# Two transformer blocks on one core: the operand buffers are given other byte offsets against the weight buffers

## The reference

```python
# first block
h = rmsnorm(x, g_mix)
z = h @ w_in                     # conv inputs, q, k, v, forget gate, two gates
merged = gc * (conv_y @ w_conv_out) + ga * (attn @ w_attn_out)
x = x + merged @ w_mix_out
u = square(relu(rmsnorm(x, g_mlp) @ w_ff1))      # 2048 -> 8192
x = x + u @ w_ff2                                # 8192 -> 2048
# second block; shift, scale and gate come from silu(c) @ w_ada
h = rms_norm(x, norm_mix_g) * (1 + scale_m) + shift_m
proj = h @ w_in2                 # q, k, v, and the state-space inputs
x = x + gate_m * (concat([rms_norm(attn), ssm]) @ w_out)
h = rms_norm(x, norm_ffn_g) * (1 + scale_f) + shift_f
g, val = split(causal_dwconv(h @ w_up))          # 2048 -> 2 x 5632
x = x + gate_f * ((silu(g) * val) @ w_down)      # 5632 -> 2048
out = rms_norm(x, g)
```

## Time and profile before

| | |
|---|---|
| median of 3 runs | 2510.3 us (2510.05 to 2511.0) |
| the profiled execution | 2512.08 us, of which the span of its instructions is 2510.2 us |
| PE busy | 2488.5 us, 99% of the span |
| PEld busy | 2164.7 us, 86% |
| DVE, ACT busy | 1972.7 us (79%), 1265.8 us (50%) |
| granted TensorE clock | 0.998 of full speed |
| DMA | 567.01 MB, 226 GB/s over the span |

### The profile page before, as it was taken

How to read it: one execution, slowest core, us unless ns; L and a number is a source line. 1 busy time by engine, 2 the same in 40 slices (tenths; PEclk the granted TensorE clock), 3 DMA queues, 4 the chain that set the end, 5 groups by cost and what they waited for, 6 DMA issues and landing times.

```text
span 2510.2 us, 46915 instructions
## 1 busy us (share of the span) xinstructions
PE 2488.5 (99%) x14373; PEld 2164.7 (86%) x14373; DVE 1972.7 (79%) x3113; ACT 1265.8 (50%) x2038; POOL 91.3 (4%) x109
## 2 busy tenths in 40 slices
PE   8999999999999999999999999999999999999998
PEld 7888888888888888888888888888888888888887
DVE  7778776689887887887888877776886886886886
ACT  5344445565554454444555555564544444445455
POOL 0000001000000000000000105300000000000000
PEclk9999999999999999999999999999999999999999
DMA  7786785557888888888888555545556556556554
GB/s 275 268 273 208 268 276 187 196 185 262 281 284 283 278 281 287 280 282 283 280 283 271 168 174 188 186 163 188 165 180 190 198 177 195 190 173 208 188 168 164
DMA packets 162668, 567.01 MB, mean 226 GB/s; under 512 B 18867, under 2 KB 19180, under 8 KB 162604
## 3 DMA queue, kind: packets, MB, share of 16 engines
q1 hardware_dynamic: 132428, 458.91, 55.0%
q10 hardware_dynamic: 27792, 101.20, 12.2%
q0 software_dynamic: 2384, 6.09, 0.9%
HBM read 563.70 MB, written 2.42 MB: 226 GB/s over the span
## 4 chain that ended last, share of the span: by engine, by line
PE 83%; DVE 1%; ACT 0%; issue 0%; DVEq 0%; ACTq 0%
PE bank L301 82%; DVE w_lo L1305 0%; ACT w_hi L788 0%; DVE scratch L1338 0%; PE bank L643 0%; PE bank L511 0%; DVE Z L2008 0%; ACT G L1117 0%; DVE scratch L1816 0%; PE bank L588 0%; DVE G L1788 0%; DVE scratch L1704 0%; PE bank L502 0%; ACT L1117 0%; ACT L827 0%
## 5 line engine op out<-in xcount | busy, mean ns | idle before, releaser
L301 PE MATMUL bank<-H,w_hi 128*128 128x512 f32 (+1 forms) x4480 | 1411.9, 394 | 12.1 <-DVE w_lo L1367 10.1
L1305 DVE TENSOR_TENSOR w_lo<-w_raw,w_hi 128x1024 fp32r<-128x1024 f32 (+2 forms) x898 | 1047.9, 1176 | 129.0 <-ACT w_hi L788 118.9
L301 PEld LDWEIGHTS bank<-H,w_lo 128*128 128x128 f32 x4416 | 832.6, 189 | 191.1
L788 ACT ACTIVATE w_hi<-w_raw 128x1024 fp32r<-128x1024 f32 (+2 forms) x898 | 876.2, 1013 | 15.5 <-PE bank L301 9.5
L301 PE MATMUL bank<-H,w_lo 128*128 128x256 f32 x4416 | 873.6, 279 | 0.0
L301 PEld LDWEIGHTS bank<-H,w_hi 128*128 128x128 f32 x4480 | 690.5, 189 | 17.8 <-issue 14.6
L301 PE MATMUL bank<-U,w_hi 128*128 128x512 f32 (+1 forms) x2011 | 626.4, 392 | 0.0
L818 ACT ACTIVATE scratch<-bank 128x256 f32<-128x256 f32 x355 | 136.2, 384 | 741.0 <-PE bank L301 740.7
L301 PEld LDWEIGHTS bank<-U,w_lo 128*128 128x128 f32 x1984 | 371.8, 188 | 83.8
L301 PE MATMUL bank<-U,w_lo 128*128 128x256 f32 x1984 | 395.5, 278 | 0.0
L301 PEld LDWEIGHTS bank<-U,w_hi 128*128 128x128 f32 x2011 | 308.5, 189 | 3.1 <-DVE w_lo L1305 0.2
(11 more groups left out here) (243 smaller groups left out, 1118.9 us busy)
## 6 DMA issues: line engine op xcount, KB each, us to landing
w_raw<-in_w_ff SPq DMA_DIRECT2D x256, 512.0 KB, 5.1
ada_w<-in_w_ada ACTq DMA_DIRECT2D x192, 512.0 KB, 4.6
w_raw<-in_w_up SPq DMA_DIRECT2D x176, 512.0 KB, 4.2
w_raw<-in_w_z SPq DMA_DIRECT2D x96, 512.0 KB, 4.9
w_raw<-in_w_in SPq DMA_DIRECT2D x88, 512.0 KB, 4.2
w_raw<-in_w_gate SPq DMA_DIRECT2D x64, 512.0 KB, 4.5
w_raw<-in_w_down SPq DMA_DIRECT2D x64, 384.0 KB, 3.1
w_raw<-in_w_down SPq DMA_DIRECT2D x64, 320.0 KB, 3.4
```

The lines of the kernel that those rows point to most:

```text
L301: return nc.tensor.matmul(out, lhsT, rhs, start=start, stop=stop, skip_group_check=True)
L788: A(w_hi[:, slot, 0:cols], w_raw[:, slot, 0:cols], ACT.Copy).then_inc(sem("w_high"), 1)
L1305: TT(w_lo[:, slot, 0:cols], w_raw[:, slot, 0:cols], w_hi[:, slot, 0:cols].bitcast(F32), ALU.subtract)\
```

## The change

The arena grows from 8 to 24 spare elements (32 to 96 bytes), `base` loses its 32 bytes, and a tensor of 24 elements (96 bytes) that nothing uses is put between H and the weight buffers. The whole diff:

```diff
-        base = (nc.sbuf_base + 31) // 32 * 32 + 32
-        ctx.enter_context(nc.sbuf_tensor("arena", [P, NC * 2 * T + Z_BLOCKS * T + 8], F32))
+        base = (nc.sbuf_base + 31) // 32 * 32
+        ctx.enter_context(nc.sbuf_tensor("arena", [P, NC * 2 * T + Z_BLOCKS * T + 24], F32))
...
         H = sb("H", [P, NC, 2 * T], F32R)
+        sb("spacing", [P, 24])
         w_raw = sb("w_raw", [P, 4, PIECE])
```

## The result

The changed kernel takes 2517.01 us (median of 13 runs, 2515.14 to 2517.66) where the kernel before takes 2510.26 (13 runs, 2509.38 to 2511.84). The ratio is 1.0024 with a 95% interval of 1.0015 to 1.0032: slower by 6.75 us. The forecast was 2503, faster. The 13 runs of either kernel lie within 2.5 us of each other, not within the 0.5 us named at the start; the difference is clear of that.

A forecast was written before the change was run, and what follows sets the result against it. PE's matmul-to-matmul pace was taken as the bound. A gain of 7 us from loads kept apart, all other terms 0, carried to the median gave 2510.3 - 7 = 2503 us; the 8-of-10 range was 2475 to 2530.

The forecast's parts named there:

- What bounds the kernel: Whole span: PE runs matmul after matmul, so only the distance between starts matters; 696.9 ns a period, 2371 of 2510 us.
- the first part of the change: Weights' load beside the operand's stream on PE: offsets 32 or 64 keep them apart, 5.7 us gained, taken as 7.
- equal offsets, as now, look like the worst case: Argument against the slower rival: offset 0 between operand and weights seemed worst for PE's two streams; no size given.
- The size of the gain: Normal periods at 696.9 ns against 695.6 from the narrow-weights group: 1.3 ns each over 3402 periods, 4.4 us.
- the 4.1 ns: Dense stretches, all matmuls of 256 columns: a full load over the whole stream costs 120.0 - 115.9 ns a matmul.
- The case on the other side: Rival: at each period's two low matmuls, loads and stream meet more often; 28 us, 2538, or 2528 for H alone; chance 0.23.
- The sign that the prediction named for each buffer deciding by itself: In the changed timeline, U and H differing by over 2 ns a period would keep the faster-stream rival alive.
- The faster stream for U and B: Rival: the operand's stream speeds up for U and B at a multiple of 128; up to 70 us, 2475 at half; chance 0.10.
- No difference by the two ports: Rival: offsets change nothing in PE's pace; the skill's independent ports would make the gain 0 us; 2510, chance 0.33.
- ACT, DVE and DMA at nothing: Other engines and DMA: new addresses cost 0 us, since PE covers DVE's work and waits for no DMA.

## Why the prediction was wrong

**What bounds the kernel** was right: the pace of PE's starts, untouched by the other engines. It holds after the change too, and it speaks against a collision of PE's reads with the writes of the weight halves: in the changed kernel the stretches of two periods of H in which DVE is busy under a tenth of the time (26 of them) have 703.4 ns a period, those in which it is busy over nine tenths (1073) 704.2, and by ACT in the same way 704.0 and 704.3; with all operands at 64 it is 690.0 and 690.3 by DVE. The sum by periods gives every one of the timed kernels within 2 us.

**The step that failed** is the first part of the change, "If other offsets keep the two streams apart, the gain is 3402 x 1.3 = 4.4 us": it gave 32 and 64 the same effect, in the same direction, for all 3402 periods, and took -7 us for the whole. The runs show a pattern of period 256 bytes, with 697.0 ns at 0, gains of 6.5 and losses of 7.7 ns around it. Within 256 bytes H went to 160 (+7.1 ns, +15.5 us) and U and B to 64 (-6.4 ns, -7.9 us), and H has 64% of the periods. That "equal offsets, as now, look like the worst case" was argued, not read from a row, and is wrong: four of the other seven distances are as slow or slower.

**The size of the gain** was bounded from the wrong group. The narrow weights stood for a stream without loads, at 695.6 ns for a period's columns; but with full loads at distance 64 the period is 690.4, below that floor. The narrow group has distances of its own (H against `wn`, whose chunks of 16 columns are 64 bytes apart, so that four distances within 256 take turns), and in the changed kernel, with others, it moved:

```profile
103.19 3.85 PE L302 MATMUL bank<-H,wn 128*16 128x512 f32 x16
106.88 0.40 PE L302 MATMUL bank<-H,w_hi 128*128 128x512 f32 x1
```

3.69 / 16 = 230.6 ns, where 231.9 was said to stay. Nor were the 4.1 ns the price of a full load beside 256 columns: in the kernel before, the two low matmuls of a period of H have such a load beside them too, and their starts are 114.8 and 115.9 ns apart, no more than the 115.9 that stood for no load. So the 120.0 ns belong to those stretches and not to a load as such; why, no run shows.

**The case on the other side** had the place and the size nearly right: more time at the low matmuls. It priced H alone at 8.2 ns a period and 2528; the run with H alone measured 6.9 ns and 2525.5. In the changed kernel the low pair of H took 118.8 + 117.4 ns, 5.5 more than before, the high pair 1.6 more. That loads and stream meet more often is not shown, only that their distance decides, and the price came from the dense stretches, so its closeness is luck. But the case had a chance of 0.23, and none was given to H and U going opposite ways, though the change gives them different distances. The sign that the prediction named for each buffer deciding by itself, H and U more than 2 ns apart, is what came.

**The faster stream for U and B** came for U and B (7.9 us of its "up to 70"), but not for its reason: place does not matter, as H at place 0 with the pace of before shows.

**No difference by the two ports.** The Trainium skill ("TensorE: Matmul & The Clock Gate", Part 2) says that loading the next weights takes no bandwidth from the running matmul. The runs differ from a load that is free at any address: with the same instructions the period of H goes from 690.4 to 704.7 ns with nothing but the distance between the two addresses. Whether it is read bandwidth that is lost, no run shows.

**ACT, DVE and DMA at nothing** was right. The halves of the weights take DVE, before and after:

```profile
L1305 DVE TENSOR_TENSOR w_lo<-w_raw,w_hi 128x1024 fp32r<-128x1024 f32 x770 | 935.9, 1224 | 121.6 <-ACT w_hi L788 116.3
```
```profile
L1306 DVE TENSOR_TENSOR w_lo<-w_raw,w_hi 128x1024 fp32r<-128x1024 f32 x770 | 935.3, 1223 | 126.0 <-ACT w_hi L789 121.0
```

**Open.** What in SBUF or PE makes the 256 bytes was not tried, nor why one distance has two paces in two products, nor steps finer than 32 bytes. The best period, 690.4 ns, is still 50 ns above one column a cycle of 2.4 GHz; no run tells why.

## What to carry to other kernels

Where PE is the bound and its starts have a steady pace, measure that pace per operand buffer: an address was worth 0.8% here against the kernel before, and left no wait in any view. Keep streamed buffers and weight buffers at one measured distance (here 64 bytes within 256, the same for both halves of the weights), measure it again where the order of the matmuls is another, and check each buffer by its own period, since a net result near zero can hide a gain and a loss. When a bound on an unknown is taken from a neighbouring group, ask first whether that group has the same unknown in it.

## What the runs showed of the hardware

With fp32r operands of 128 partitions, the distance between the starts of matmuls depends on (operand address - weight address) within 256 bytes, at the eight steps of 32 bytes from 690.3 to 704.7 ns for 1536 columns in four matmuls, as means over a buffer. It did not change with the operand's place at the same distance (H at 0 and at 32: 697.1 and 697.0 ns), and by at most 1 ns with DVE idle or busy beside it (H, 703.4 and 704.2; 690.0 and 690.3). Two products with the same buffers at the same distance can differ (U at distance 128: 697 ns in one, 703 in the other). The fastest step, 64, takes 0.8% off the kernel against distance 0 (ratio 0.9916, 0.9902 to 0.993).
